# Two chunks on one stationary side in the level products of a gated linear recurrence

## What is computed

```python
q = silu(hg_q);  f = lb + (1 - lb) * sigmoid(hg_f);  k = 1 - f;  v = hg_i
G = cumsum(log(f))                      # within a chunk
A[t, s] = sum_d q[t, d] * exp(G[t, d] - G[s, d]) * k[s, d]     # s <= t
o = A @ v + (q * exp(G)) @ S
S = exp(G_last) * S + (k * exp(G_last - G)).T @ v
```

## Time and profile before

| | |
|---|---|
| time, median of 3 runs | 711.09 us (710.65 to 711.4) |
| profiled execution, its own time | 710.82 us |
| its span | 709.1 us |
| instructions | 13457 |
| TensorE products / weight loads busy | 694.0 us (98%) / 665.5 us (94%) |
| VectorE (DVE) / ScalarE (ACT) / GpSimd (POOL) busy | 434.0 / 308.3 / 357.1 us |
| granted TensorE clock | 0.998 of full |

### The profile page before, as it was taken

The page is one execution under the profiler, slowest core; times in us unless marked ns, Lnnn a source line. Parts: engine busy times, 40 slices in busy tenths (PEclk is TensorE's granted clock), DMA queues, the critical chain, the costliest instruction groups (busy, mean ns, idle before and its releaser), DMA issues.

```text
span 709.1 us, 13457 instructions
## 1 busy us (share of the span) xinstructions
PE 694.0 (98%) x4822; PEld 665.5 (94%) x4822; DVE 434.0 (61%) x1006; ACT 308.3 (43%) x860; POOL 357.1 (50%) x475
## 2 busy tenths in 40 slices
PE   7999999999999999999999999999999999999995
PEld 6799999999999999999999999999999998888884
DVE  6845346369892364598933635989426258776257
ACT  6644541634544425445545254445443253232333
POOL 5773233257672432376824242768343558765423
PEclk9999999999999999999999999999999999999999
DMA  7356243321123447450739331202244315211014
GB/s 264 40 62 92 17 47 74 35 31 31 30 40 52 64 73 37 19 43 16 42 53 73 67 42 27 34 10 49 54 68 157 86 46 201 80 56 55 29 45 193
DMA packets 63989, 44.93 MB, mean 63 GB/s; under 512 B 17438, under 2 KB 59044, under 8 KB 63924
## 3 DMA queue, kind: packets, MB, share of 16 engines
q1 hardware_dynamic: 63924, 44.07, 35.9%
HBM read 35.82 MB, written 7.65 MB: 61 GB/s over the span
## 4 chain that ended last, share of the span: by engine, by line
PE 90%; DVE 4%; POOL 2%; issue 2%; ACT 1%; DMA 0%; SPq 0%; DVEq 0%; POOLq 0%; ACTq 0%
PE proj L278 48%; PE proj L297 9%; PE mix L2174 7%; PE mix L1728 5%; PE mix L2172 3%; PE mix L1759 3%; PE mix L1709 2%; PE mix L846 1%; PE mix L904 1%; PE mix L1703 1%; PE mix L895 1%; PE mix L910 1%; PE mix L830 1%; PE mix L1699 1%; PE mix L1698 1%
## 5 line engine op out<-in xcount | busy, mean ns | idle before, releaser
L278 PE MATMUL proj<-uTh,w_high 128*128 128x352 f32 (+4 forms) x768 | 260.9, 340 | 0.0
L278 PE MATMUL proj<-uTh,w_low 128*128 128x352 f32 (+4 forms) x768 | 245.8, 320 | 0.0
L278 PE MATMUL proj<-uTl,w_high 128*128 128x352 f32 (+4 forms) x768 | 245.2, 319 | 0.0
L278 PEld LDWEIGHTS proj<-uTh,w_high 128*128 128x128 f32 x768 | 145.1, 189 | 0.2
L278 PEld LDWEIGHTS proj<-uTl,w_high 128*128 128x128 f32 x768 | 145.0, 189 | 0.0
L278 PEld LDWEIGHTS proj<-uTh,w_low 128*128 128x128 f32 x768 | 144.3, 188 | 0.0
L323 POOL TENSOR_TENSOR w_low<-w_raw,w_high 128x256 fp32r<-128x256 f32 (+1 forms) x54 | 72.2, 1338 | 53.3 <-DVE decay L371 26.8
L1300 POOL TENSOR_TENSOR f_suffix<-f_suffix,f_prefix 128x192 f32<-128x192 f32 x84 | 54.5, 649 | 25.1 <-DVE f_prefix L1520 17.6
L1728 PEld LDWEIGHTS mix<-level_x 128*127 128x127 f32 (+6 forms) x448 | 54.3, 175 | 5.3 <-issue 2.9
L1728 PE MATMUL mix<-level_x 128*127 128x64 f32 (+6 forms) x448 | 54.1, 253 | 0.8 <-DVE level_x L1511 0.8
L1568 DVE SCALAR_TENSOR_TENSOR conv_out<-conv_in,hg_taps,conv_out 128x352 f32<-128x352 f32 (+2 forms) x81 | 52.4, 647 | 0.5
(11 more groups left out here) (307 smaller groups left out, 1391.3 us busy)
## 6 DMA issues: line engine op xcount, KB each, us to landing
w_raw<-in_w_in SPq DMA_DIRECT2D x32, 512.0 KB, 8.4
x_tile<-in_x SPq DMA_DIRECT2D x8, 512.0 KB, 6.1
w_raw<-y_scratch SPq DMA_DIRECT2D x8, 384.0 KB, 4.2
decay<-gamma_scratch SPq DMA_DIRECT2D x4, 576.0 KB, 4.0
landing<-in_w_out SPq DMA_DIRECT2D x4, 512.0 KB, 7.7
landing<-in_x SPq DMA_DIRECT2D x3, 512.0 KB, 6.2
out_y<-landing SPq DMA_DIRECT2D x3, 512.0 KB, 2.6
y_scratch<-gd_y SPq DMA_DIRECT2D x6, 192.0 KB, 1.8
```

The lines of the kernel that those rows point to most:

```text
L278: last = pe.matmul(acc[:, 0:tw], w[j % 2][:, k, :], u[:, k, t0:t0 + tw], start=(k == 0 and i == 0), stop=(k == KT - 1 and i == 2))
```

## The change

Chunks 1 and 2 of a group share one stationary side. Chunk 1's keys lie in the even blocks of a 128-column tile, as before; chunk 2's keys are written in reverse order of tokens into the odd blocks, which were queries until now. The queries go to a tile of their own (`XQ`, 64 columns a chunk, packed), and one product of 128 by 128 columns serves both chunks; chunk 0 keeps a product of its own, with all 128 columns as stationary side. Since the scores of chunk 2 then have their keys in reverse order, its `hg_k` for the diagonal, its `hg_v` and its part of `hg_kf` are reversed too: ScalarE writes `back` twice a group, and TensorE waits for it (`k_back`, `v_back`). The masks become one set for each chunk of a group (`mask_odd`, `mask_diag`), the reversed ones made by POOL in the front stage: `flipped_masks`, two memsets, 15 `affine_select`s and two copies, between `early_low(3)` and `early_low(4)`. ScalarE's squares go to `on`, since `sq` is gone.

The hunks below stand in the order front stage (POOL, VectorE), then `phase_hg`: POOL, ScalarE, VectorE, TensorE.

```diff
+        def flipped_masks():
...
+            pool.memset(flipped[:, 0:LEVELS, :], 1.0).then_inc(flip_step, 1)
+            pool.memset(flip_diag, 0.0).then_inc(flip_step, 1)
...
+            pool.tensor_copy(mask_odd[:, :, GC - 1, :], flipped[:, 0:LEVELS, :])
+            pool.tensor_copy(mask_diag[:, GC - 1, :], flip_diag)
...
-        dve.tensor_copy(mask_st[:, 1:LEVELS + 1, :], mwork[:, 0:LEVELS, :])
+        for i in range(LEVELS):
+            b = 1 << i
+            odd = mwork[:, i, :].rearrange("p (n two b) -> p n two b", two=2, b=b)[:, :, 1, :]
+            for c in range(GC - 1):
+                dve.tensor_copy(mask_odd[:, i, c, :].rearrange("p (n b) -> p n b", b=b), odd)
...
+            for t in XK:
+                pool.memset(t[:, 0:P], 0.0)
...
+                    if i:
                         pool.wait_ge(suf_done, n)
-                        pool.tensor_tensor(xv_[:, :, 0, :], kv_[:, :, 0, :], sv_[:, :, 0, :], ALU.mult
-                                           ).then_inc(x_even, 1)
+                    flipped_k = XK[n % 2][:, P:2 * P][:, ::-1]
+                    for dst, cs in ((XK[n % 2][:, first(g):2 * P], slice(first(g), 2 * P)), (flipped_k, slice(2 * P, GW))):
+                        xv_, kv_, sv_ = (halves(t, b)[:, :, 0, :] for t in (dst, kk[:, cs], suf[:, cs]))
+                        if i == 0:
+                            last = pool.tensor_copy(xv_, kv_)
+                        else:
+                            last = pool.tensor_tensor(xv_, kv_, sv_, ALU.mult)
+                    last.then_inc(x_even, 1)
...
-                pool.tensor_tensor(kf[:, :], kk[:, :], suf[:, :], ALU.mult).then_inc(kf_done, 1)
+                pool.tensor_tensor(kf[:, 0:2 * P], kk[:, 0:2 * P], suf[:, 0:2 * P], ALU.mult)
+                pool.tensor_tensor(kf[:, 2 * P:GW][:, ::-1], kk[:, 2 * P:GW], suf[:, 2 * P:GW], ALU.mult).then_inc(kf_done, 1)
...
+                if g:
+                    full(act, plan, ("ty", g - 1))
-                    last = act.activation(sq[:, chunk(i)], o[:, chunk(i)], ACT.Square,
+                    last = act.activation(on[:, chunk(i)], o[:, chunk(i)], ACT.Square,
...
             for g in range(NG):
+                act.wait_ge(fk, g + 1)
+                if g:
+                    full(act, plan, ("tv", g - 1))
+                act.copy(back[:, :], kk[:, 2 * P:GW][:, ::-1]).then_inc(k_back, 1)
                 for m in range(LEVELS + 1):
                     take(("gram", g, m))
+                    if m == 0:
+                        full(act, plan, ("gram", g, 0))
+                        act.copy(back[:, :], hv[:, (g + 1) * GW - P:(g + 1) * GW][:, ::-1]).then_inc(v_back, 1)
...
-                dve.tensor_tensor(xv_[:, :, 1, :], qv_[:, :, 1, :], pv_[:, :, 1, :], ALU.mult).then_inc(x_odd, 1)
+                dve.tensor_tensor(XQ[n % 2][:, lo // 2:GW // 2].rearrange("p (n b) -> p n b", b=b),
+                                  qv_[:, :, 1, :], pv_[:, :, 1, :], ALU.mult).then_inc(x_odd, 1)
...
+                    if m == 0:
+                        pe.wait_ge(k_back, g + 1)
+                        for i in live(g):
+                            last = pe.matmul(ap[:, chunk(i)], kk[:, chunk(i)] if i < GC - 1 else back[:, :], hq[:, g * GW + i * P:g * GW + (i + 1) * P],
                                              start=True, stop=True)
-                            both = X[(LEVELS * g + m - 1) % 2][:, chunk(i)]
-                            keys = max(P - (1 << (m - 1)), HALF)
-                            last = pe.matmul(ap[0:keys, i * P // 2:(i + 1) * P // 2], both[:, 0:keys],
-                                             halves(both, 1 << (m - 1))[:, :, 1, :], start=True, stop=True)
+                    else:
+                        n = LEVELS * g + m - 1
+                        keys, odd = XK[n % 2], XQ[n % 2]
+                        if g:
+                            pe.matmul(ap[:, 0:P // 2], keys[:, 0:P], odd[:, 0:P // 2], start=True, stop=True)
+                        last = pe.matmul(ap[:, P // 2:GW // 2], keys[:, P:2 * P], odd[:, P // 2:GW // 2], start=True, stop=True)
...
+                pe.wait_ge(v_back, g + 1)
+                turn("tv", g, lambda i: hv[:, g * GW + i * P:g * GW + (i + 1) * P] if i < GC - 1 else back[:, :])
```

More of the change, by code:

```diff
@@ L537, in level_masks @@
                 pool.wait_ge(mask_step, 2 * i + 1 + cut)
+        def flipped_masks():
+            pool.memset(flipped[:, 0:LEVELS, :], 1.0).then_inc(flip_step, 1)
+            pool.memset(flip_diag, 0.0).then_inc(flip_step, 1)
+            pool.wait_ge(flip_step, 2)
+            cells = lambda i: flipped[:, i, :].rearrange("p (n b) -> p n b", b=1 << i)
+            for i in range(LEVELS):
+                b = 1 << i
+                pool.affine_select(out=cells(i), in_=cells(i), compare_op=ALU.is_ge, fill=0.0, base=b - P,
+                                   pattern=[[2 * b, P // (2 * b)], [0, b]], channel_multiplier=1).then_inc(flip_step, 1)
+            pool.affine_select(out=flip_diag, in_=flip_diag, compare_op=ALU.not_equal, fill=1.0,
+                               base=1 - P, pattern=[[1, P]], channel_multiplier=1).then_inc(flip_step, 1)
+            pool.wait_ge(flip_step, LEVELS + 3)
+            for i in range(LEVELS):
+                b = 1 << i
+                pool.affine_select(out=cells(i), in_=cells(i), compare_op=ALU.is_ge, fill=0.0, base=P - 1,
+                                   pattern=[[-2 * b, P // (2 * b)], [0, b]], channel_multiplier=-1).then_inc(flip_step, 1)
+            pool.wait_ge(flip_step, 2 * LEVELS + 3)
+            pool.tensor_copy(mask_odd[:, :, GC - 1, :], flipped[:, 0:LEVELS, :])
+            pool.tensor_copy(mask_diag[:, GC - 1, :], flip_diag)
         for i in range(AHEAD):
@@ L1033, in phase_hg @@
         kk = sb("hg_k", [P, GW], F32, st)
-        X = [sb(f"level_x{i}", [P, GW], F32, st) for i in range(2)]
+        XK = [sb(f"level_k{i}", [P, 2 * P], F32, st) for i in range(2)]
+        XQ = [sb(f"level_q{i}", [P, GW // 2], F32, st) for i in range(2)]
+        back = sb("hg_back", [P, P], F32, st)
         A = [sb(f"hg_scores{i}", [P, GC, P], F32, st) for i in range(2)]
```

34 lines of the change are left out of this document (13 added, 21 removed).

## The result

| | before | after |
|---|---|---|
| median of the runs | 711.25 us (710.65 to 711.46) | 719.23 us (718.82 to 721.93) |
| ratio | | 1.0118, interval 1.0106 to 1.0130 |
| span of the profiled execution | 709.1 us | 717.0 us |
| granted TensorE clock, mean | 0.998 | 0.995 |

After is 8.0 us slower, where 3.1 were forecast; 719.23 lies 0.2 us above the range. The direction was right.

What follows compares the result with a forecast made beforehand. TensorE was taken as the bound, except POOL in first groups of heads 0 to 2. Gain -8.3, POOL +2.7 and waits +8.7 us sum to +3.1: 713.9 us, or 714.2 against the median; range 706.0 to 719.0.

Steps and rivals of the forecast that it cites:

- The stalls: Third groups' starts: TensorE waits for ScalarE's late copy into `back`, 2.35 us in three heads, 1.7 in the last, +8.7 us.
- the wait in the first groups: Heads 0 to 2: TensorE waits 0.4 us for `back`, hidden because the levels behind wait for POOL and DVE.
- TensorE's saving: Level loops: four full-width loads replace six, two replace four in first groups; TensorE's work falls by 13.1 us.
- What of it becomes time in heads 0 to 2: Second and third groups gain four fifths of 6.2 us, 5.0 us; first groups, where POOL sets the pace, gain nothing.
- The price of POOL: Even half in two operations: +0.13 us a level, paid in full in first groups of heads 0 to 2, 2.7 us.
- Elsewhere TensorE covers it: Outside the first groups of heads 0 to 2, POOL's extra time for the split even half costs nothing.
- The rival that named 719.2: DVE and POOL become the bound in all groups of heads 0 to 2; the 5.0 us gain vanishes; chance 0.13.
- The rule on shared SBUF interfaces: POOL's 10.9 us of new time would be lost on DVE wherever it falls, giving 722.4 us; the forecast rejected it.
- Free parts: Front stage: POOL's flipped masks, some 7 us, hide in a 10.23 us wait; DVE's extra casts, 2 us, in idle time.
- The second piece of `hg_kf`: End of each group: adds 0.13 us on POOL, which ends its levels before TensorE does.

Runs made afterwards that it cites:

- hoist: The kernel after, with ScalarE's reversed copy of `hg_k` for groups 2 and 3 moved up, right behind the copy of `hg_ktok`: 710.86 us.
- before_pe: The kernel before with TensorE's part alone, one product for chunks 1 and 2 (chunk 2's scores use chunk 1's keys): 705.9 us.
- before_pe_split: `before_pe` with POOL's even half of a level in two operations, both forward: 711.72 us.
- before_split: The kernel before with POOL's even half of a level in two operations, both forward, and nothing else: 715.18 us.
- hoist_order: `hoist` with third-group POOL root and VectorE's `gd_y` earlier, `w_low` quarters later; `hg_kf`'s reversed piece first, no dead chunk in head 3: 708.35 us.
- last_only: The kernel before with the change in head 3 alone, reversed `hg_k` copies made early and `hg_kf`'s reversed piece first: 708.88 us.
- before_copy: The kernel before with only ScalarE's late reversed copy of chunk 2 of `hg_k`, into `sq`, and TensorE's wait for it: 721.11 us.

## Why the prediction went wrong, step by step

**The stalls: right.** 8.7 us were forecast and 8.8 stand in the trace. The order of ScalarE's operations came as read from the trace of before, and the wait in the first groups was hidden, as forecast. That the early copy takes away 8.4 us, so near to 8.8, is partly luck, as told under `hoist`. The half clock behind the first stall, some 1.6 us, was in no term of the sum.

**TensorE's saving: right in size.** Four loads stand where six stood, and in head 3 a group is 0.95 to 1.1 us shorter where 1.04 and 1.2 were worked out. Weight loads of after in head 0's second group, 0.49 us from the first to what follows:

```profile
176.29 0.35 PEld L1775 LDWEIGHTS mix<-level_q,level_k 128*128 128x128 f32 x2
176.56 0.30 PEld L1776 LDWEIGHTS mix<-level_q,level_k 128*128 128x128 f32 x2
176.78 0.30 PEld L941 LDWEIGHTS mix<-gd_u,gd_kd 128*128 128x128 f32 x2
```

**What of it becomes time in heads 0 to 2: the step that failed.** I took four fifths, 5.0 us, from the idle time of DVE in a window. Even with nothing else changed it is 2.0 (second groups 1.64, third 0.39, `before_pe`), and with POOL's split it is none (`before_pe_split`: second groups +0.6, third +0.9 in all). A window's idle time says that an engine could do more. It does not say where in the list the next wait lies. In the third groups that was a chain over four engines. It keeps TensorE's load idle for 0.90 us a head in `before_pe`, of which the trace of before shows 0.19. In the second groups it was the load behind `gd_o`, 0.33 us a head, of which before shows nothing.

**The price of POOL: mis-sized, and put in the wrong place.** 0.13 us a level was an extrapolation of the shortest durations down to 64 columns; measured are 0.27. The split costs 3.8 us by itself and 5.8 beside the faster TensorE, where 2.7 were taken. "Elsewhere TensorE covers it" was wrong: `before_split` pays more in second groups (1.98 us) than in first (1.74). In the first groups the two errors went against each other. Twice the price a level, paid in seven levels, would be 1.9 us a group; measured are 0.6, two levels' worth, in after as in `before_split`. So POOL sets the pace there in some of the levels only, and the term of 2.7 us is 1.8 there, and what is missing from it stands in the second groups.

**The rival that named 719.2** had POOL and DVE as the bound in all groups of heads 0 to 2. It named what came: nothing gained in second and third groups. Its place was right only in part: in the third groups it was the order of steps, which `hoist_order` mends without taking work from either engine. That its number is met to 0.03 us is luck, since 1.6 us of the measured time are the half clock, which it did not have.

**VectorE beside POOL.** The rule on shared SBUF interfaces gave 722.4. POOL has 32.1 us more, VectorE's busy time grew by 2.6; the odd halves of three chunks take 621 ns in the mean against 610, those of two chunks 323 against 463. The extensions of `f_prefix` take 574 ns against 536. So by the busy times the GPSIMD Engine Reference's rule (the Trainium skill, section 1. Specifications) did not turn POOL's 32.1 us into as much time of VectorE; what VectorE lost in one operation it won in another. No run shows its operations without POOL beside them.

**Free parts: right.** Front stage and masks (`last_only`). POOL's flipped masks took 10.2 us, 63.55 to 73.78, not 7, and just filled the idle time of 10.23; `w_low` behind them starts at 73.85 against 74.07. A few more masks would not have been free. **The second piece of `hg_kf`** is not free in head 3: TensorE waits 0.42 us for it, and the start of the second group is 0.64 us later (0.36 in `last_only`, with the other order).

**Left open.** The rest of -0.5 us in the table lies outside the level loops: -0.4 in the front, +0.7 between heads 0 and 1, -0.65 between heads 1 and 2. Kernels that change nothing there show 0.0 to +1.2 between heads 0 and 1 (`before_split` 0.0, `last_only` +0.4, `before_pe` +1.2), so it may be a matter of single profiles; no run settles it. That the half clock follows from the stall rests on two kernels with it and twelve without; why only the first of four stalls did so isn't known.

## What to carry to other kernels

A wait that you add costs what stands ahead of its producer in that engine's list, so put the producer where its input becomes ready; here that was 8.4 us for one moved line. Before you count a saving of the bound engine as time, look in each stretch for the chain of small steps that ends closest to it, and move the earliest step, not the reader: moving the reader only passed the wait on. Splitting an operation of POOL costs a fixed 0.3 us at this size, so share a stationary side only where POOL has room, or keep its work in one piece, which only `before_pe` does here, without the right scores for chunk 2.

## What the hardware showed that I had not expected

A POOL operation of 64 columns takes 430 ns in the mean, one of 128 547 and one of 192 694. Writing in reverse order has no price that shows: in `hoist` 72 of the 96 pieces of 64 columns are written backwards, and their mean is 440 ns; in `before_pe_split`, all forward, 445.

The clock: after 2.3 us in which TensorE was idle, the granted clock stayed full for 1.3 us and then was 0.50 for 3.41 us, with TensorE fully busy (195.09 to 198.51 in after, 194.48 to 197.89 in `before_copy`); it cost some 1.6 us. The equal stalls of heads 1 and 2 and the shorter one of head 3 were followed by no such stretch in these two profiles. Nor need it be the same in each execution: of the four of after, three had a mean clock of 0.995 or 0.996, and the fourth had 0.990 and took 721.93 us. The Trainium skill, TensorE: Matmul & The Clock Gate, Part 1, says that the half rate is the resting state and activity lifts it; the trace agrees in that an idle stretch came first, and the three later stalls, of 2.3 us or less, without a drop show that an idle stretch alone does not decide it.
